# Hybrid decoder step on one core: attention pipelined one block deeper, convolution taps redistributed, recurrence started inside the attention's tail

## What is computed

```python
proj = h @ W['w_in'][l]                       # 7680 columns: 60 units of 128
# A) gated linear recurrence (4 heads of 128), B) stick-breaking attention (8 heads of 64),
# C) causal depthwise convolution of 31 taps, and 24 units of gate logits
z = einsum('bhqd,bhkd->bhqk', q, k) * (SB_HEAD_DIM ** -0.5) + bias
log_rest = where(mask, log_sigmoid(-z), 0.0)
tail = lax.cumsum(log_rest, axis=3, reverse=True) - log_rest
A = where(mask, exp(log_sigmoid(z) + tail), 0.0)
o = einsum('bhqk,bhkd->bhqd', A, v)
```

## Time and profile before

| | us |
|---|---|
| time, median of 3 runs (lowest, highest) | 2382.62 (2382.07, 2383.61) |
| time of the profiled execution | 2382.67 |
| its span, first to last instruction | 2380.9 |
| TensorE busy | 2086.1 (88%) |
| VectorE, ScalarE, GpSimd busy | 1101.2, 610.0, 591.3 |
| mean granted TensorE clock | 0.941 |

### The profile page before, as it was taken

The page is one execution under the profiler, slowest core; times in us unless marked ns, Lnnn a source line. Parts: engine busy times, 40 slices in busy tenths (PEclk is TensorE's granted clock), DMA queues, the critical chain, the costliest instruction groups (busy, mean ns, idle before and its releaser), DMA issues.

```text
span 2380.9 us, 32200 instructions
## 1 busy us (share of the span) xinstructions
PE 2086.1 (88%) x12832; PEld 1984.5 (83%) x12832; DVE 1101.2 (46%) x1169; ACT 610.0 (26%) x792; POOL 591.3 (25%) x392
## 2 busy tenths in 40 slices
PE   7898789977999779997787989879999999999994
PEld 5887688867888678886787889759999999999993
DVE  3267465664547655566543653362223222222235
ACT  3234322344134342334312522130101001001011
POOL 1211211121111112111212232242333332323332
PEclk9999899988999889998898999889999999999997
DMA  4221203111031111310225331311111111111121
GB/s 138 61 82 31 66 19 117 49 36 57 19 120 46 36 57 37 119 36 27 75 83 184 109 122 47 123 69 41 40 57 31 48 52 32 53 40 40 57 104 77
DMA packets 203987, 156.89 MB, mean 66 GB/s; under 512 B 15730, under 2 KB 188402, under 8 KB 203890
## 3 DMA queue, kind: packets, MB, share of 16 engines
q1 hardware_dynamic: 201698, 146.89, 19.7%
q10 hardware_dynamic: 2192, 8.65, 0.9%
HBM read 120.16 MB, written 35.35 MB: 65 GB/s over the span
## 4 chain that ended last, share of the span: by engine, by line
PE 68%; DVE 18%; ACT 6%; issue 5%; DMA 1%; SPq 1%; POOL 0%; POOLq 0%; DVEq 0%; ACTq 0%
PE psum L367 59%; DVE arena L1284 3%; PE psum L671 2%; DVE arena L1256 2%; DVE arena L1282 1%; DVE arena L1257 1%; PE psum L604 1%; PE psum L572 1%; DVE hid L1523 1%; DVE arena L1272 1%; PE psum L653 1%; DVE ug L1285 1%; DVE mix L1508 1%; PE psum L626 1%; DVE arena L1285 1%
## 5 line engine op out<-in xcount | busy, mean ns | idle before, releaser
L367 PE MATMUL psum<-h_hi,w_hi 128*128 128x352 f32 x2400 | 557.2, 342 | 157.3 <-ACT gate_logits L895 61.2
L367 PEld LDWEIGHTS psum<-h_hi,w_hi 128*128 128x128 f32 x2400 | 416.8, 197 | 184.6 <-issue 163.4
L367 PE MATMUL psum<-h_lo,w_hi 128*128 128x352 f32 x2400 | 533.9, 332 | 0.0
L367 PE MATMUL psum<-h_hi,w_lo 128*128 128x352 f32 x2400 | 530.7, 330 | 0.0
L367 PEld LDWEIGHTS psum<-h_lo,w_hi 128*128 128x128 f32 x2400 | 425.5, 196 | 0.0
L367 PEld LDWEIGHTS psum<-h_hi,w_lo 128*128 128x128 f32 x2400 | 424.4, 194 | 0.0
L344 POOL CAST w_hi<-w_raw 128x1024 fp32r<-128x1024 f32 x60 | 71.8, 1197 | 967.5 <-PE psum L367 948.6
L357 POOL CAST w_hi<-w_raw 128x512 fp32r<-128x512 f32 (+1 forms) x128 | 96.5, 754 | 736.6 <-PE psum L367 642.0
L359 POOL TENSOR_TENSOR w_lo<-w_raw,w_hi 128x512 fp32r<-128x512 f32 (+1 forms) x128 | 227.8, 1780 | 10.3
L1173 ACT ACTIVATE hid<-psum 128x1056 f32<-128x1056 f32 x32 | 33.7, 1054 | 583.1 <-PE psum L367 583.1
L367 PE MATMUL psum<-hid_hi,w_hi 128*128 128x352 f32 x768 | 166.4, 325 | 10.8 <-DVE hid_lo L1525 10.8
(11 more groups left out here) (237 smaller groups left out, 2417.9 us busy)
## 6 DMA issues: line engine op xcount, KB each, us to landing
w_raw<-in_w_in SPq DMA_DIRECT2D x60, 512.0 KB, 4.1
w_raw<-in_w_ff SPq DMA_DIRECT2D x32, 512.0 KB, 4.0
w_raw<-in_w_ff SPq DMA_DIRECT2D x64, 256.0 KB, 2.7
g_d<-gate_logits SPq DMA_DIRECT2D x24, 528.0 KB, 3.1
gates<-g_d SPq DMA_DIRECT2D x24, 528.0 KB, 3.6
arena<-in_xT SPq DMA_DIRECT2D x8, 528.0 KB, 7.3
x_again<-in_xT SPq DMA_DIRECT2D x1, 4224.0 KB, 13.8
x_d<-x_again ACTq DMA_DIRECT2D x8, 528.0 KB, 2.7
```

The lines of the kernel that those rows point to most:

```text
L367: mm = pe.matmul(ps[:, b0 + g, 0:GW], w[:, slot, k, :], x[:, k, g * GW:(g + 1) * GW], start=(k == 0 and w is wh and x is xh), stop=(k == k ...
```

## The change

1. **Scores one block ahead.** TensorE makes the scores of block q+1 in block q; ScalarE reads them before it makes the weights of block q. The loop has 8 iterations, with 3+2+3 steps. The unit of block q is copied out behind the weights.
2. **Tail and recurrence.** What was iteration 8 becomes `T_FILL` steps between the last transposes and values, and ScalarE's Abs/Exp/Ln and sigmoids of the recurrence stand between its last attention copies. One sigmoid goes to another buffer.
3. **Steps in the recurrence.** Eight steps precede the first level, and all levels have some; before, the last two had none. None stand behind the norm's product at the group's end any more.
4. **Taps.** `TAPS[q]` gives how many taps stand ahead of and behind the two tail sums; before it was one each at four places of a block. `clip` does both heads together. `stage_unit(13)` moves ahead of the norm. The order of SP's and GpSimd's lists is as before.

```diff
 QB = TP // P
 Z_CHUNKS = [q if q < 4 else 4 + 2 * (q - 4) for q in range(QB + 1)]
-A_FILL = (2, 2, 3, 1)
-H_FILL = (4, 4, 3, 3, 3, 3, 3, 3, 3, 3, 4, 4)
+A_FILL = (3, 2, 3)
+T_FILL = (2, 2, 2, 2)
+L_FILL = (8, 3, 3, 2, 3, 3, 2, 4)
+H_FILL = (4, 4, 4)
...
+                scores(p, 0, 0)
                 turn9(vT, 5).then_inc(v_turned.sem, 1)
-                for q in range(QB + 1):
-                    if q < QB:
-                        scores(p, q, 0)
+                for q in range(QB):
                     if q == 1:
                         v_staged.wait(pe, p, 1)
                     if q:
                         turn_a(p, 2 * q - 2)
+                    if q + 1 < QB:
+                        scores(p, q + 1, 0)
                     fill(A_FILL[0])
-                    if 4 <= q < QB:
-                        scores(p, q, 1)
                     if q == 1:
                         sample_scores(p)
                     if q == 3:
                         sample_turn(p)
+                    if q:
+                        turn_a(p, 2 * q - 1)
+                    fill(A_FILL[1])
+                    if 4 <= q + 1 < QB:
+                        scores(p, q + 1, 1)
                     if q == 4:
...
-                    fill(A_FILL[1])
-                    if q:
-                        turn_a(p, 2 * q - 1)
-                    fill(A_FILL[2])
...
                         values(p, q - 1)
-                    fill(A_FILL[3])
-
+                    fill(A_FILL[2])
+
+
+                turn_a(p, 14)
+                fill(T_FILL[0])
+                turn_a(p, 15)
+                fill(T_FILL[1])
+                values(p, QB - 1)
+                fill(T_FILL[2])
...
-                fill(H_FILL[0])
+                fill(T_FILL[3])
...
-                fill(H_FILL[1])
                 for j in range(NL):
+                    fill(L_FILL[j])
...
-                    if j < 5:
-                        fill(H_FILL[2 + j])
-                fill(H_FILL[7])
+                fill(L_FILL[NL])
...
-                fill(H_FILL[9])
...
-                fill(H_FILL[10])
...
+                fill(H_FILL[2])
...
-                fill(H_FILL[11])
...
+                stage_unit(13, p, more)
...
-                stage_unit(13, p, more)
...
+                def clip(q):
+
+                    n = P * (q + 1)
+                    for e in range(2):
+                        z_read.wait(dve, p, 2 * Z_CHUNKS[q + 1] - 1 + e)
+                        dg = zb[2 * (q % 2) + e][:, q * P:n]
+                        ch.mark(dve.tensor_tensor(dg, dg, neg, ALU.add))
                     ch.wait()
-                    dve.tensor_scalar(l, z, ZMAX, None, ALU.min).then_inc(e_ready.sem, 1)
+                    for e in range(2):
+                        dve.tensor_scalar(lb[e][:, 0:n], zb[2 * (q % 2) + e][:, 0:n], ZMAX, None, ALU.min)\
+                            .then_inc(e_ready.sem, 1)
...
                 for q in range(QB):
-                    scores_read(q, 0)
-                    scores_read(q, 1)
+                    clip(q)
...
-                    tap()
+                    taps_of(TAPS[q][0])
                     tail_sum(q, 0)
-                    tap()
                     tail_sum(q, 1)
...
-                while taps[0] < CW:
...
-                    tap()
-
-
+                    taps_of(TAPS[q][1])
+
+
+                taps_of(CW)
...
 
+                av_done.wait(dve, p, QB)
+                os_done.wait(dve, p, 1)
```

ScalarE's loop, as it now stands, and its tail:

```diff
+                now_set.wait(act, p, 2)
+                read_scores(0)
+                v_turned.wait(act, p, 1)
...
+                for q in range(QB):
+                    softplus(q, 0)
...
+                    softplus(q, 1)
...
+                    if q:
+                        stage_at(q - 1, 1)
+                    if q == 0:
+                        u_ready.wait(act, p, 1)
+                    if q + 1 < QB:
+                        read_scores(q + 1)
...
+                        read_values(q - 1)
+                    weights_of(q, 0)
+                    weights_of(q, 1)
+                    stage_unit(q, p, more)
+
+
+                stage_at(QB - 1, 0)
...
-                arg_ready.wait(act, p, 16)
+                stage_at(QB - 1, 1)
                 act.activation(A(B_W[0], T), qA[:, :], ACT.Sigmoid)
-                act.activation(A(B_W[1], T), gA[:, :], ACT.Sigmoid)
+                act.activation(A(B_KD, T), gA[:, :], ACT.Sigmoid)
                 act.activation(A(B_KK, T), fT[:, :], ACT.Sigmoid, scale=-1.0).then_inc(sig_ready.sem, 1)
                 lnexp()
+                read_values(QB - 1)
+                if more:
+                    kv_stored.wait(act, p, 32)
+                stage_unit(8, p, more)
                 ia_turned.wait(act, p, 1)
```

More of the change, by code:

```diff
@@ L932, in group, with read_scores @@
                 ch = Chain(act, a_seq, p * CHAIN_A + 1)
-                v_turned.wait(act, p, 1)
-                act.activation(vtok[:, 0:1024], banks(5, 1024), ACT.Copy)
-                act.activation(vtok[0:SM, 1024:1152], ps[0:SM, 7, 0:P], ACT.Copy).then_inc(v_staged.sem, 1)
-                now_set.wait(act, p, 2)
-                def read_scores(q, c):
-                    z_ready.wait(act, p, Z_CHUNKS[q] + c + 1)
-                    n = min(512, P * (q + 1) - 512 * c)
-                    for e in range(2):
-                        act.activation(zb[2 * (q % 2) + e][:, 512 * c:512 * c + n], bank(3 + e, n), IDN,
-                                       bias=sbp[:, e:e + 1]).then_inc(z_read.sem, 1)
+                def read_scores(q):
+                    for c in range(Z_CHUNKS[q + 1] - Z_CHUNKS[q]):
+                        z_ready.wait(act, p, Z_CHUNKS[q] + c + 1)
+                        n = min(512, P * (q + 1) - 512 * c)
+                        for e in range(2):
+                            act.activation(zb[2 * (q % 2) + e][:, 512 * c:512 * c + n], bank(3 + e, n), IDN,
+                                           bias=sbp[:, e:e + 1]).then_inc(z_read.sem, 1)
                 def softplus(q, e):
@@ L966, in stage_at, with read_values @@
                     act.activation(atv[e][:, 0:n], banks(5, n), ACT.Copy).then_inc(at_ready.sem, 1)
-                for q in range(QB + 1):
-                    if q:
-                        stage_unit(q - 1, p, more)
-                    if q < QB:
-                        if q == 1:
-                            u_ready.wait(act, p, 1)
-                        read_scores(q, 0)
+                def read_values(q):
+                    av_done.wait(act, p, q + 1)
+                    if q == 0:
+                        oa_stored.wait(act, p, 0)
+                    act.activation(ob[:, q * P:(q + 1) * P], ps[:, 7, (q % 4) * P:(q % 4 + 1) * P],
+                                   ACT.Copy).then_inc(o_read.sem, 1)
+                now_set.wait(act, p, 2)
+                read_scores(0)
+                v_turned.wait(act, p, 1)
+                act.activation(vtok[:, 0:1024], banks(5, 1024), ACT.Copy)
+                act.activation(vtok[0:SM, 1024:1152], ps[0:SM, 7, 0:P], ACT.Copy).then_inc(v_staged.sem, 1)
+                for q in range(QB):
+                    softplus(q, 0)
                     if q:
                         stage_at(q - 1, 0)
-                    if 4 <= q < QB:
-                        read_scores(q, 1)
-                    if q < QB:
-                        softplus(q, 0)
+                    if q == 3:
+                        args_ready.wait(act, p, 1)
+                        z = A(A_ZS, SBK, slice(0, 64))
+                        act.activation(z, z, ACT.Exp).then_inc(as_ready.sem, 1)
+                    softplus(q, 1)
                     if q == 1:
@@ L984, in group @@
                             .then_inc(zs_read.sem, 1)
-                    if q == 3:
-                        args_ready.wait(act, p, 1)
-                        z = A(A_ZS, SBK, slice(0, 64))
-                        act.activation(z, z, ACT.Exp).then_inc(as_ready.sem, 1)
-                    if q:
-                        stage_at(q - 1, 1)
-                    if q < QB:
-                        softplus(q, 1)
-                        weights_of(q, 0)
                     if q == 2:
@@ L1287, in group, with taps_of @@
                 zs, ls = A(A_ZS, SBK, slice(0, 64)), A(A_LS, SBK, slice(0, 64))
+                def taps_of(n):
+                    for _ in range(n):
+                        tap()
                 for q in range(QB):
-                    scores_read(q, 0)
-                    scores_read(q, 1)
+                    clip(q)
                     if q == 2:
```

53 lines of the change are left out of this document (17 added, 36 removed).

## The result

The changed kernel took 2221.95 us (median of 4 runs, 2218.28 to 2222.81), the kernel before 2382.35 (4 runs, 2381.94 to 2383.61): a ratio of 0.9323, 95% interval 0.9307 to 0.9339. That is 160.4 us less, where 152.4 were forecast. The profiled execution took 2222.81 with a span of 2221.0.

A forecast was written before the change was run, and what follows sets the result against it. TensorE's work and waits bound the kernel: idle and half clock lost 228.7 us in the four groups. With 76.3 left over, the gain is 152.4, so 2382.6 falls to 2230 us, range 2212 to 2248 (8 in 10: 2208 to 2268).

The forecast's parts named there:

- norm's Ln and the loop's turn: Group start: TensorE waits 1.25 us for ScalarE's Ln and 0.85 for the turn, 2.1 in each of groups 1 to 3.
- scores of block 1: Group start: TensorE waits for ScalarE's read of block 0's scores, 4.1 us in group 0, 6.9 in groups 1 to 3.
- copies of units: Blocks 1, 7 and behind 7: TensorE's other work is shorter than the 1.2 us copy, 1.1 us of wait a group.
- first levels: Recurrence's first level: TensorE waits for unit 8's copy and the copy of `iT`, 2.4 us a group against 4.0 before.
- states and squares, last group: Last group: output product waits 1.5 us for the chain of states; its 2.1 for the squares stays.
- half clock, starts: Behind the wait at block 1's scores: half clock loses 1.0 us in group 0, 2.1 in groups 1 to 3.
- half clock, sample's values: Behind the sample's values: clock stays half for 6.8 us of work, 3.4 lost a group, half of it in group 0.
- The ring: Old blocks run as one ring through three engines; block 7 takes 27.6 us with TensorE busy 19.4.
- TensorE sets the pace: All blocks run at TensorE's pace: 2230 us, in itself 2212 to 2248, chance 66%.
- Rivals 3 and 4: Rival 3: half the ring stays in blocks 5 to 7, 2296 us, 9%. Rival 4: no overlap, slower, 2403 us, 3%.
- The small transfers: Group start: last small DMA issue moves up 1.5 us; a shorter start could give no more than some 2 us.
- Rival 2: VectorE becomes the bound in iterations 2 to 6 as GpSimd holds it up: 2250 us, or 2265 with half clock; 17%.

The follow-up runs named there:

- the experiments on the two orders: Changed kernel with ScalarE's weights made before reading the next scores, 2296.72 us; or with TensorE's next scores issued behind a block's last steps, 2342.51 us.
- four versions that shortened the start: Changed kernel with steps first, 2212.14 us; store's wait later, 2215.23; both plus earlier copies of i, 2198.68; steps behind the norm and ahead of block 1's scores, 2185.7.
- the one with steps first: Changed kernel with three of block 0's steps ahead of the scores of block 1 instead of behind them: 2212.14 us.
- even taps: Changed kernel with four taps in each of blocks 0 to 6, three in block 7 and none behind: 2222.32 us.
- The extra operations: Changed kernel with two more unused 128 x 1024 VectorE operations behind the tail sums of each of blocks 1 to 7: 2234.52 us.
- the version with steps in both places: Changed kernel with four steps put back behind the norm product and three of block 0's steps ahead of block 1's scores: 2185.7 us.

## Why the prediction was right, and where it was off

The mechanism held. Each of its terms, in us over four groups, beside what the waits and windows above show:

```
                                 predicted   measured
norm's Ln and the loop's turn         6.3       11.1   (4.8, 4.8, 1.5)
scores of block 1                    24.8       19.4   (3.9, 4.0, 4.1, 7.4)
copies of units                       4.4        4.5
first levels                          9.6        9.2
states and squares, last group        3.6        3.3
half clock, starts                    7.3       12.1   (1.7, 3.2, 4.6, 2.6)
half clock, sample's values          11.9        8.5   (1.7, 1.7, 3.4, 1.7)
half clock, first levels              6.8        5.0   (1.7, 1.7, 0, 1.7)
half clock, last norm product         1.6        2.0
sum                                  76.3       75.1   (from the windows)
```

That the half clock's four terms add up to 27.6 forecast and 27.7 measured is luck: the starts were set 4.8 too low and the rest as much too high.

*The ring.* "TensorE sets the pace" is right in all blocks (the mean granted clock is 0.960, forecast 0.96), and the experiments on the two orders show that it needs the read ahead, with waits in the places and, within 0.8 us, the sizes that were expected. In ScalarE's tightest block, 7, its copy of the unit came with 1.26 us to spare (group 0), where 1.5 were forecast. Rivals 3 and 4 fall. (The prediction's 15.2 us for block 7 should be 17.3 - 2.3 = 15.0; nothing hangs on it.)

*The loop's turn* is the step that was wrong: "the loop's turn, which I put at 0.85". Group 3's instructions stand behind the loop, so that only the Ln is waited for there: 1.45. The other two waited 4.8, so a turn costs 3.3. The 0.6 and 1.1 of the earlier trace rows were what was left of it behind four queued steps, and the change took these steps away. With them back it is 0.7. The Trainium skill (Runtime: NRT & Kernel Launch, "Instruction fetch mechanics") says that a taken branch out of the fetched window makes the engine fetch its target before it can go on. The rows fit that, but no run here separates the fetch from the rest of a turn.

*The store that holds ScalarE.* Timeline of the changed kernel, group 1; the norm product ends at 343.8:

```profile
343.82 1.14 ACT L1073 ACTIVATE arena<-psum,eps 128x1056 f32<-128x1056 f32 x1 [0.81 <-PE psum L772]
...
349.53 1.05 SPq L416 DMA_DIRECT2D g_d<-gate_logits  x1
...
354.55 0.63 ACT L946 ACTIVATE arena<-psum,bias_now 128x128 f32<-128x128 f32 x2 [8.47 <-DMA g_d<-gate_logits]
...
370.06 0.33 SPq L408 DMA_DIRECT2D arena<-in_vc  x1
```

The issue came at E+5.7 (predicted 5.6), ScalarE at E+10.8 (predicted 9.9). TensorE came 2.7 later than predicted, for the turn, and so waited 4 and not 6.9. Both ends of the start were off and the start as a whole, 4.79 + 3.95 = 8.7, was not: 9.0 was predicted. That is luck, since two errors cancelled. Group 3, without a turn, waited 7.4.

*The small transfers.* The last is issued at E+26.3 (forecast 25.9), and the sample's scores begin at 375.25, E+31.5. The sentence that a shorter start "could give no more than some 2 us" is right in kind: four versions that shortened the start and left the transfers where they were waited for them, 1.5, 6.6, 9.9 and 12.5 us in all. (The version with four steps behind the norm didn't: those steps fill the start, and its sample's scores come at E+32.8.) In size it was too strict for the sum of the groups, as the one with steps first gained 9.8 us.

*GpSimd.* Two rows behind block 7, group 0, and the page's group of all the taps (busy, mean ns):

```profile
238.14 2.40 POOL L349 TENSOR_TENSOR w_lo<-w_raw,w_hi 128x1024 fp32r<-128x1024 f32 x1
238.14 3.49 DVE L1259 SCALAR_TENSOR_TENSOR arena<-arena,conv_w_now 128x1024 f32<-128x1024 f32 x1
```

```profile
L1259 DVE SCALAR_TENSOR_TENSOR arena<-arena,conv_w_now 128x1024 f32<-128x1024 f32 x120 | 158.1, 1317 | 2.2
```

A tap that began beside a subtraction took 3.49 instead of 1.28. The Trainium skill's rule (SBUF — State Buffer, "Who interferes with whom") is borne out for the taps too. But the mean of all 120 is 1.32, so they lost 4 us in all. More of the effect falls on the first operation of a tail sum (1.68 in the timeline of the result, 1.08 for the same size undisturbed), ahead of which VectorE idles (86.3 us in 28 waits of the four groups). Rival 2 failed because VectorE has room, and not for want of the effect: with even taps they lose 37 us (a mean of 1.588 against 1.281 before) and the time is the same. The extra operations show how near it was: VectorE's room ends within their 2.4 us a block.

*The part outside the sum.* Between the two profiled executions, whose spans differ by 159.9 us, 121.9 are waits of TensorE in the groups and 31.7 the clock there. That is 1.2 more than the forecast's 152.4. Two parts were not in the forecast at all. The first is the work itself, TensorE's busy time less what the half clock cost: 921.5 us in the groups before (980.9 - 59.4) and 913.9 after (941.6 - 27.7), 7.6 less for the same matmuls. The second is behind the groups, where 1.3 are given back, by windows of before and of after:

```profile
1249.80:2380.90 1131.10, 1026.29 (x6120) 1005.05 (x6120) 399.53 (x262) 186.23 (x179) 358.71 (x264) 0.96 0.22 70
```

```profile
1088.60:2221.00 1132.40, 1027.23 (x6120) 1005.72 (x6120) 399.33 (x262) 185.94 (x179) 359.28 (x264) 0.96 0.22 70
```

Of those 1.3 the clock is 1.1: TensorE is busy there at half clock for 40.4 us, before for 38.2. Of the 7.6 a part lies in how stretches of steps begin and end. Counted in the records of the groups, the first matmul of a stretch holds TensorE 0.09 us longer than a following one, and the last is shown 0.16 longer where a wait follows; 170 stretches with 24 such waits became 146 with 4. By this estimate it is 5.4 us. The ends of matmuls are modelled, no run separates this part, and the rest stays open.

## What to carry to other kernels

Where a block is a ring through three engines, issue and read the next block's input ahead of this block's last result, on both engines: with ScalarE's order undone 86 of the 160 us are left, with TensorE's undone 40, each time with everything else of the change kept. Queued work behind the last product of a loop's body pays twice, as it hides most of the loop's turn too (0.7 us left of 3.3 here), whose full size showed in the trace only when nothing was queued. When a start gets shorter, look at once for the transfer that was hidden behind it, and when transfers are moved ahead, for the one that they are now ahead of.

## What I had not expected of the hardware

The turn of the loop costs TensorE 3.3 us when nothing is queued behind the last product (4.8 against 1.45 without a turn), 0.7 with four steps queued. Idle time of 1.4 us more at one place of a group, with a full instead of a half clock at three first levels, came out at the same time (2222.32 and 2221.95). And the start without a wait at the scores also kept the full clock, and reached the small transfers sooner by both: in the version with steps in both places TensorE came to the sample's scores of group 1 at 358.7 (its wait of 3.67 ended at 362.34), 7.7 before the version with steps behind the norm alone (366.36). The removed wait is 3.8 of that and an earlier turn 1.4; the other 2.5 are a half-clock stretch of 6.8 us that only the latter has there. The last transfer was issued at 360.2, only 0.7 earlier. (The traces are of the slowest execution of the one version and the fastest of the other.)
